# Two row-major projections of a transformer block on one core: the last two chunks by token block

## The reference, cut to what matters

```python
x = x + rms_norm(memory_attention(h, m, w_mq, w_mk, w_mv, w_mo), mem_norm_post)   # ends with "@ w_mo", 1024 x 1024
h = rms_norm(x, ffn_norm_pre)
x = x + rms_norm(conv_ffn(h, w_up, conv_w, conv_b, w_down), ffn_norm_post)        # ends with "@ w_down", 2816 x 1024
...
h = concatenate([meta, x]); u = _rmsnorm(h, norm_w[0]); proj = u @ w_in           # first product of the second model
```

## Time and profile before

| What | Value |
|---|---|
| Median of 3 runs | 923.64 us (923.4 to 923.68) |
| The profiled execution | 922.43 us, of which its span is 920.7 us |
| Granted TensorE clock, mean over the span | 0.999 of full speed |
| PE busy | 908.9 us, 99% of the span |
| DVE, ACT, POOL busy | 655.7, 532.2, 131.6 us |
| Share of PE in the chain of waits that ended last | 93% |

### The profile page before, as it was taken

The page is one execution under the profiler, slowest core; times in us unless marked ns, Lnnn a source line. Parts: engine busy times, 40 slices in busy tenths (PEclk is TensorE's granted clock), DMA queues, the critical chain, the costliest instruction groups (busy, mean ns, idle before and its releaser), DMA issues.

```text
span 920.7 us, 19094 instructions
## 1 busy us (share of the span) xinstructions
PE 908.9 (99%) x6971; PEld 853.1 (93%) x6971; DVE 655.7 (71%) x1115; ACT 532.2 (58%) x904; POOL 131.6 (14%) x131
## 2 busy tenths in 40 slices
PE   8999999999999999999999999999999999999997
PEld 7998899998999998889999999999999998888886
DVE  4898877545899998447877777766578476767743
ACT  6868586545776765546444444444464567666643
POOL 2211010000056566000111111101010000000000
PEclk9999999999999999999999999999999999999999
DMA  8853434435345555652555555555355444455561
GB/s 303 278 169 109 149 109 166 158 117 184 135 161 204 197 193 207 211 203 96 190 174 179 175 174 178 171 196 180 139 184 185 159 159 135 160 166 161 182 196 56
DMA packets 44995, 157.58 MB, mean 171 GB/s; under 512 B 6067, under 2 KB 7219, under 8 KB 44684
## 3 DMA queue, kind: packets, MB, share of 16 engines
q1 hardware_dynamic: 44380, 155.03, 49.4%
q0 software_dynamic: 560, 1.79, 0.7%
HBM read 155.74 MB, written 1.06 MB: 170 GB/s over the span
## 4 chain that ended last, share of the span: by engine, by line
PE 93%; DVE 3%; ACT 2%; issue 1%; DMA 1%; SPq 0%; DVEq 0%; ACTq 0%
PE acc L1311 13%; PE acc L1313 13%; PE acc L1312 13%; PE scores L1311 6%; PE scores L1313 6%; PE scores L1312 6%; PE acc L1264 4%; PE acc L1266 4%; PE acc L1265 4%; PE scores L1265 2%; PE scores L1266 2%; PE scores L1264 2%; PE outs L1266 2%; PE outs L1264 2%; PE outs L1265 2%; PE acc L1395 1%
## 5 line engine op out<-in xcount | busy, mean ns | idle before, releaser
L1884 DVE TENSOR_TENSOR w_lo<-raw,w_hi 128x1024 fp32r<-128x1024 f32 x287 | 353.4, 1238 | 97.0 <-ACT w_hi L665 96.5
L665 ACT ACTIVATE w_hi<-raw 128x1024 fp32r<-128x1024 f32 x287 | 301.3, 1056 | 150.4 <-PE acc L1313 62.7
L1311 PE MATMUL acc<-XH,w_hi 128*128 128x256 f32 (+1 forms) x616 | 176.2, 286 | 0.5 <-DVE Y L2431 0.3
L1312 PE MATMUL acc<-XL,w_hi 128*128 128x256 f32 (+1 forms) x616 | 173.5, 282 | 0.0
L1313 PE MATMUL acc<-XH,w_lo 128*128 128x256 f32 (+1 forms) x616 | 173.5, 282 | 0.0
L1311 PE MATMUL scores<-XH,w_hi 128*128 128x272 f32 (+1 forms) x424 | 120.1, 283 | 0.0
L1313 PE MATMUL scores<-XH,w_lo 128*128 128x272 f32 (+1 forms) x424 | 119.7, 282 | 0.0
L1312 PE MATMUL scores<-XL,w_hi 128*128 128x272 f32 (+1 forms) x424 | 119.7, 282 | 0.0
L1311 PEld LDWEIGHTS acc<-XH,w_hi 128*128 128x128 f32 x616 | 115.9, 188 | 3.0 <-issue 2.4
L1312 PEld LDWEIGHTS acc<-XL,w_hi 128*128 128x128 f32 x616 | 116.0, 188 | 0.1
L1313 PEld LDWEIGHTS acc<-XH,w_lo 128*128 128x128 f32 x616 | 115.9, 188 | 0.0
(11 more groups left out here) (539 smaller groups left out, 1801.7 us busy)
## 6 DMA issues: line engine op xcount, KB each, us to landing
raw<-weights SPq DMA_DIRECT2D x287, 512.0 KB, 3.4
cst<-params SPq DMA_DIRECT2D x1, 1080.5 KB, 10.7
XR<-x_t SPq DMA_DIRECT2D x2, 512.0 KB, 6.1
Y<-mem_t SPq DMA_DIRECT2D x1, 1024.0 KB, 9.6
AR<-bias_rows POOLq DMA_DIRECT2D x4, 256.0 KB, 5.4
out<-AR SPq DMA_DIRECT2D x2, 512.0 KB, 2.6
AR<-final_gain POOLq DMA_DIRECT2D x1, 512.0 KB, 6.1
AR<-lgate_w POOLq DMA_DIRECT2D x1, 192.0 KB, 2.6
```

Source lines behind the costliest of these rows:

```text
L665: nc.scalar.activation(w_hi[:, n % SLOTS, :], raw[:, n % SLOTS, :], ACT.Copy).then_inc(hi_ready, 1)
L1311: nc.tensor.matmul(o, wh, h, start=start, stop=False)
L1312: nc.tensor.matmul(o, wh, l, start=False, stop=False)
L1884: V.tensor_tensor(w_lo[:, s, :], raw[:, s, :], w_hi[:, s, :].bitcast(F32), ALU.subtract).then_inc(lo_ready, 1)
```

## The change

It has five parts, in the memory output and in the down projection alike.

1. **PE, last two chunks by block.** Of the second half's last two chunks, block 0's twelve products are made first, then block 1's twelve. `rows_half` rises behind block 0's. `chunk_done` of both chunks is raised in block 1's part.
2. **PE, the two matmuls of `keep_warm(WARM, PTB)` between the products and the transposes are gone** (4 records of the profile for each stage). The two behind the transposes stay.
3. **ACT, `hi` of the chunk three behind the stage's last** (the next stage's third chunk) stands behind block 0's root instead of ahead of block 0's squares.
4. **POOL makes the low part of that chunk** (`lo_behind`) in place of DVE; DVE hands it on with a one-column memset that raises `lo_ready`. In the down projection it stands ahead of the gate weights' loading on POOL's queue.
5. **DVE adds tiles 0 and 1 of the residual by block**: block 0's 128 columns as soon as they are turned (`first_turned`), ahead of block 1's reciprocal, and block 1's 128 columns behind it. Two semaphores are merged with others.

```diff
--- before.py
+++ after.py
@@ -341,8 +341,9 @@
         rf_zero, sum_ready, cmp_hidden, cmp_copied, rest_pool = (
             sem("rf_zero"), sem("sum_ready"), sem("cmp_hidden"), sem("cmp_copied"), sem("rest_pool"))
         rel_loaded = sem("rel_loaded")
-        gate_loaded, gate_scaled, gate_summed, l_gate_summed, gate_parted = (
-            sem("gate_loaded"), sem("gate_scaled"), sem("gate_summed"), sem("l_gate_summed"), sem("gate_parted"))
+        first_turned, behind_lo = sem("first_turned"), sem("behind_lo")
+        gate_scaled, gate_summed, gate_parted = (
+            sem("gate_scaled"), sem("gate_summed"), sem("gate_parted"))
         token_rstd, shifted, rf_ready, rf_hi, gate_exp, swapped = (
             sem("token_rstd"), sem("shifted"), sem("rf_ready"), sem("rf_hi"), sem("gate_exp"),
             sem("swapped"))
@@ -609,6 +610,15 @@
 
             sum_squares(lambda m: wait_evacuated(pool, TILE["w_out"] + m), META)
 
+            def lo_behind(name, per):
+
+                n = CHUNK[name] + 2 * per - 1 + AHEAD
+                w = n % SLOTS
+                pool.wait_ge(hi_ready, n + 1)
+                nc.gpsimd.tensor_tensor(w_lo[:, w, :], raw[:, w, :], w_hi[:, w, :].bitcast(F32), ALU.subtract).then_inc(behind_lo, 1)
+
+            lo_behind("mo", 4)
+
             def ffn_pool(p, i, hidden, rest):
                 pool.wait_ge(f_gelu, p + 1 + 2 * i)
                 pool.wait_ge(u_tapped, 2 * p + 2 + 4 * i)
@@ -622,8 +632,9 @@
             for p in range(16, FFN_TILES):
                 ffn_pool(p, 0, ffn_hi(p), ffn_lo(p))
 
-            pool.dma_start(lgate_raw, lgate_w).then_inc(gate_loaded, 16)
-            pool.wait_ge(gate_loaded, 16)
+            lo_behind("down", FFN_TILES // 2)
+            pool.dma_start(lgate_raw, lgate_w).then_inc(row_loaded, 16)
+            pool.wait_ge(row_loaded, 16)
             w = grouped(lgate_raw)
             nc.gpsimd.tensor_tensor(w, w, col("g_mlstm", 0, KT).unsqueeze(2).to_broadcast([P, KT, STRIP]), ALU.mult).then_inc(gate_scaled, 1)
             for v in (gA, gA_tail, rstd_m[:, S:T]):
@@ -720,7 +731,7 @@
             def rows_norm(name, u, per):
 
                 n, t = CHUNK[name], TILE[name]
-                for c in range(2 * per):
+                for c in range(2 * per - 1):
                     ahead(n + c)
                     if c == per:
                         wait_chunk(act, n + per - 1)
@@ -732,6 +743,7 @@
                     if b == 0:
                         act.wait_ge(rows_half, u + 1)
                     else:
+                        ahead(n + 2 * per - 1)
                         wait_chunk(act, n + 2 * per - 1)
                     chain.link(nc.scalar.activation(sqv[:, span(2 + b, 512)], SC[:, span(b, 512)], ACT.Square,
                                                     accum_out=row_sq2[:, b:b + 1]))
@@ -1061,7 +1073,7 @@
             for m in range(KT):
                 ahead(CHUNK["lq"] + m)
                 if m == 0:
-                    act.wait_ge(l_gate_summed, 1)
+                    act.wait_ge(gate_summed, 2)
                     nc.scalar.activation(gx[0:36, :], OB[1][0:36, 0:T], ACT.Identity, bias=col("gate_b")[0:36]).then_inc(g_raw, 1)
                     act.wait_ge(g_raw, 1)
                     chain.link(nc.scalar.activation(ge[32:36, :], gx[32:36, :], ACT.Abs))
@@ -1270,7 +1282,7 @@
                 t = TILE[name]
                 for half in range(2):
                     o = [acc(t + b)[:, :] if half == 0 else SC[:, span(b, 512)] for b in range(2)]
-                    for c in range(per):
+                    for c in range(per if half == 0 else per - 2):
                         n = CHUNK[name] + per * half + c
                         pe.wait_ge(lo_ready, n + 1)
                         if half == 0:
@@ -1280,10 +1292,18 @@
                                 pe.wait_ge(evacuated[(t + b) % 2], (t + b) // 2)
                             for j in (2 * c, 2 * c + 1):
                                 last = rows_product(n, o[b], x, j, b, j == 2 * per - 1, j == 0)
-                            if half and b == 0 and c == per - 1:
-                                last.then_inc(rows_half, 1)
                         last.then_inc(chunk_done, 1)
-                keep_warm(WARM, PTB)
+                for b in range(2):
+                    for c in (per - 2, per - 1):
+                        n = CHUNK[name] + per + c
+                        if b == 0:
+                            pe.wait_ge(lo_ready, n + 1)
+                        for j in (2 * c, 2 * c + 1):
+                            last = rows_product(n, o[b], x, j, b, j == 2 * per - 1)
+                        if b:
+                            last.then_inc(chunk_done, 1)
+                    if b == 0:
+                        last.then_inc(rows_half, 1)
                 for b in range(2):
                     for k in range(KT):
                         if b == 0 and k == 0:
@@ -1297,6 +1317,8 @@
                         last = nc.tensor.transpose(turned_rows(k)[:, b * P:(b + 1) * P], y_rows[:, b, k * P:(k + 1) * P], ident[:, :])
                         if b and k % 2:
                             last.then_inc(rows_turned, 1)
+                        elif k == 1:
+                            last.then_inc(first_turned, 1)
                 keep_warm(WARM_SPREAD)
 
             def begin(n, t, first, i=0, depth=2):
@@ -1732,7 +1754,7 @@
                     stat_sum(NORM_H1, 2, lambda: pe.wait_ge(sq_ready, SQ_H1 + KT), T)
                 if m == 3:
                     pe.wait_ge(gate_parted, 1)
-                    nc.tensor.matmul(OB[1][:, 0:T], lgate_raw[:, KT * STRIP:KT * STRIP + P], lgate_parts, start=True, stop=True).then_inc(l_gate_summed, 1)
+                    nc.tensor.matmul(OB[1][:, 0:T], lgate_raw[:, KT * STRIP:KT * STRIP + P], lgate_parts, start=True, stop=True).then_inc(gate_summed, 1)
             for m in range(KT):
                 chunk(CHUNK["lq"] + m, TILE["lq"] + m, l_in(AH, META), l_in(AL, META), S, ready=h1_ready if m == 0 else None)
                 if m == 6:
@@ -1959,8 +1981,18 @@
             def rows_update(name, u, update, post, pre, a):
 
                 t = TILE[name]
+
+                def add_block(k, b):
+                    cols = slice(META + b * P, META + (b + 1) * P)
+                    return V.scalar_tensor_tensor(out=XR[:, k, cols], in0=turned_rows(k)[:, span(b, P)], scalar=col(post, k),
+                                                  in1=XR[:, k, cols], op0=ALU.mult, op1=ALU.add)
+
                 for b in range(2):
                     rstd_b = row_rstd[:, b:b + 1]
+                    if b:
+                        dve.wait_ge(first_turned, u + 1)
+                        for k in (0, 1):
+                            add_block(k, 0)
                     dve.wait_ge(rows_root, 2 * u + b + 1)
                     V.reciprocal(rstd_b, row_root[:, b:b + 1]).then_inc(rows_rstd, 1)
                     dve.wait_ge(rows_rstd, 2 * u + b + 1)
@@ -1974,8 +2006,11 @@
                     V.scalar_tensor_tensor(out=XR[:, k, META:T], in0=turned_rows(k), scalar=col(post, k), in1=XR[:, k, META:T],
                                            op0=ALU.mult, op1=ALU.add).then_inc(x_updated, 1)
 
-                add(0)
-                add(1)
+                dve.wait_ge(rows_turned, 4 * u + 1)
+                for k in (0, 1):
+                    add_block(k, 1).then_inc(x_updated, 1)
+                dve.wait_ge(behind_lo, u + 1)
+                V.memset(small[:, 159:160], 0.0).then_inc(lo_ready, 1)
                 for k in range(KT):
                     if k + 2 < KT:
                         add(k + 2)
@@ -2599,7 +2634,7 @@
                 if c == 1:
                     l_lo(LHEADS - 1)
                 if c == 10:
-                    dve.wait_ge(row_loaded, 16)
+                    dve.wait_ge(row_loaded, 32)
                     dve.wait_ge(half_squared, 2)
                     chain.note(V.tensor_scalar(small[:, 44:46], small[:, 40:42], 1.0 / D, EPS, ALU.mult, ALU.add))
                     for b in range(2):
```

## The result

| | median of the runs | ratio to the kernel before, interval |
|---|---|---|
| before | 923.5 us (22 runs, mostly 922.85 to 924.18) | |
| changed | 927.57 us (22 runs, 923.07 to 929.85) | 1.0025, 1.0013 to 1.0037 |

The kernel became slower by 0.25%, where 0.06% faster was forecast, and 927.57 us lies outside the range. (The ratio weighs all runs; that of the two medians alone would be 1.0044.) Both numbers hide something: the changed kernel's 22 times stand in two groups with nothing in between, nine from 923.07 to 923.74 (median 923.33) and thirteen from 927.46 to 929.85 (median 927.81). The profiled execution, 927.71 us with a span of 926.0, is of the upper group.

A forecast was written before the change was run, and what follows sets the result against it. The prediction took PE, busy 99% of the span, as the bound. Gains of 0.15 and 0.13 us made 0.27 us per seam, 0.54 us for two, taking 923.64 to 923.1 us; range 922.2 to 924.4.

The forecast's parts named there:

- signs of being right: Both seams about 3.5 us, hole 0.7 to 1.0, reciprocal 0.04 behind root, POOL's low part 2.3 to 3.0 us.
- signs of being wrong: PE's first product released by DVE's memset or POOL, clock below 1.00 at either seam, or a seam under 3 us.
- What bounds the kernel: Whole kernel: PE is busy 99% of the span, so gains must come from PE's own instructions or idle time.
- Order of the products, keep_warm, hole: Seam: block 0's transposes begin 0.88 us earlier, leaving a hole before block 1's; by themselves these 0.88 us give nothing.
- Reciprocal 0.15 us earlier: Seam, block 1: DVE is free sooner, so its reciprocal and PE's transposes come 0.15 us earlier.
- Additions by block 0.13 us: Seam's end: half-tile additions bring ACT's high part forward, meeting the second keep_warm's end; first product another 0.13 us earlier.
- The sum 0.27 for each seam: Memory output and down projection: next stage's first product on PE comes 0.27 us earlier in each.
- POOL's low part, 2.7 us: Seam: POOL's 1024-column subtraction takes 2.7 us, free of DVE contention, over before DVE needs it.
- Rival A: Seams: POOL's subtraction late at 6.6 us, PE starts 3.0 us later in each, 929.6 us; chance 6%.
- Gate weights behind it: Down projection: POOL's gate-weight work may delay DVE by up to 0.74 us, covered by 1.3 us, nothing on the path.
- Rival B: Seams: clock falls to half in the new hole, 1.9 us lost in each, 926.9 us; chance 3%.
- are all that the change can move: Memory output and down projection: only the stretches from PE's last product to next stage's first, 3.78 us, can change.

The follow-up runs named there:

- experiment 8: Changed kernel with the two short keep_warm matmuls between products and transposes put back; 927.74 us, ratio 1.0033.
- 11: Changed kernel plus a one-column POOL memset behind the memory output's low part, minus the two keep_warm matmuls behind the transposes; 922.7 us, ratio 0.9993.
- 1: Kernel before plus one idle one-column POOL memset ahead of the feed-forward loop; 924.38 us, ratio 1.0021.
- 3: Changed kernel with the memory output's low part back on DVE and its residual additions by whole tile; 922.84 us, ratio 0.9995.
- 5: Changed kernel plus one idle one-column POOL memset behind the memory output's low part; 923.0 us, ratio 0.9996.
- 9: Kernel before plus two idle one-column POOL memsets ahead of the feed-forward loop; 923.41 us, ratio 0.9998.
- 2: Kernel before without the one short keep_warm matmul pair ahead of the feed-forward loop; 927.21 us, ratio 1.0037.
- 6: Changed kernel plus three idle one-column POOL memsets behind the memory output's low part; 927.26 us, ratio 1.0038.
- 7: Changed kernel with both moved low parts on DVE and residual tiles added whole; 923.34 us, ratio 1.0001.
- 10: Repeat of the changed kernel plus one idle one-column POOL memset behind the memory output's low part; 922.64 us, ratio 0.9992.
- 4: Changed kernel plus one short keep_warm matmul pair in the feed-forward's third round, two rounds written out; 927.09 us, ratio 1.0048.

## Why the prediction was wrong

None of the prediction's signs of being right failed, and none of its signs of being wrong appeared: they all lie in the seams, and the seams did what they were to do. The time was lost elsewhere.

*What bounds the kernel.* Right, and not followed to its end: at 99% on PE's line, whatever makes a thousand matmuls 4% longer outweighs a seam. I read idle time and clock, and took a matmul's duration as fixed by its form.

*Order of the products, keep_warm, hole.* Right: block 0's transposes follow directly, hole 0.93 us (0.7 to 1.0 forecast). "By themselves they give nothing" was wrong: experiment 8 shows 0.13 us in each seam. The working of the 0.15 us used additions at 229.22, which the seam only has without keep_warm, so the sum held and the share was booked to the wrong part.

*Reciprocal 0.15 us earlier.* Measured 0.15 at the transposes (1.98 against 2.13 us behind the last product), reciprocal 0.04 us behind the root. *Additions by block 0.13 us.* Measured 0.13 to 0.14 (3.63 against 3.50). *The sum 0.27 for each seam*: measured 0.28 and 0.27. The argument that the second keep_warm's end meets the high part made no difference: without it the seam is the same (11).

*POOL's low part, 2.7 us.* Measured 2.36 and 2.35, so the 2.7 was 0.34 us too long, and the four pieces of 256 columns behind it (2.95) 0.59. The estimate from the Trainium skill's "GPSIMD Engine Reference", section "3.1 Elementwise — side-by-side cycle accounting", 2.25 us, was 0.11 too short and so nearer. Nobody waits for it. Rival A did not occur.

*Gate weights behind it.* Right: PE's three chunks behind the down seam last 9.05 us before and after, and DVE's first low part keeps its distance from the seam (429.58 - 423.78 = 424.30 - 418.50 = 5.80).

*Rival B.* The clock is 1.00 in the seam. It did not occur either, though its price of some 4 us came, by another way and at another place.

**The failed step** is the sentence that the seam and its twin "are all that the change can move", and with it the part "The low part on POOL": the instruction was costed by its duration and its neighbours in the seam, and then taken as free. That instruction also shifts the loop behind it in POOL's stream. POOL's second multiplication of the loop comes 0.33 us late, the order at the shared port turns, DVE's low part takes 1.77 us instead of 1.22, and PE waits 0.6 us (shown by experiments 1, 3, 5 and 9). Behind the wait 13 of 22 executions, by their times, ran on in the 117.8 ns rhythm and lost about 4 us more (2 and 6 show that price without the 0.6 us wait). No rival had this chain. The other nine, median 923.33 us, lie near the 923.1 forecast by luck: the seams' 0.55 us and a wait of 0.6 would cancel (no profile shows one of the nine). Where the wait is avoided, the rest of the prediction stands: 923.0 and 922.64 us against the 923.1 forecast.

Not settled: what POOL does in the 0.33 us. Fetching of instructions would be a guess, and the one thing the traces hold on it does not decide: each has a single 8 KB load on the instruction queue q14 in these rounds (for which engine, it does not say), and it starts 4.2 us behind POOL's first multiplication in the kernel before and in the changed one alike, 2.7 us behind it in experiments 5 and 9.

Not settled either: what decides the rhythm behind an interruption. After the wait of 0.6 us 13 of 22, 4 of 12 and 4 of 7 runs were in the upper group (changed kernel, 1, 8), after 0.1 us 5 of 5 (6); without a wait 1 of 66 (3, 5, 7, 9, 10, 11) and 3 of 96 of the kernel before. Experiments 2 and 4 were there in all 5 runs each, 2 without a wait and 4, in its profile, behind the added pair.

## What to carry to other kernels

Where one engine's line is the whole time, count what it does per microsecond in a long stretch before and after (matmuls in a window), not only its gaps: a matmul's pace is not fixed by its shape, and a short interruption can cost far more than its length. An instruction that is put ahead of a loop on a side engine is not free because it is hidden where it stands; look at the first rounds of the next loop for who gets the shared port. Signs of being right or wrong that all lie where the edit is cannot catch such a loss: name one for the stretches in between. And where a time falls into two groups, try the kernel with one idle instruction more before judging the idea.

## What the hardware showed that I had not expected

- Back-to-back 256-column matmuls, each with its weight load, have two rhythms at a granted clock of 1.00: 113.3 and 117.8 ns. Either can last over 100 us (444 against 427 matmuls in 50 us), and in the profiles it changes at an interruption: a wait of 0.1 or 0.6 us, or a short pair, which left the shorter rhythm at one place and the longer one at another.
- One more instruction on POOL, even a one-column memset some 20 us ahead of a loop, makes one step of the loop's first rounds 0.33 us late; two do not; four (the low part and three memsets) make another step 0.38 us late.
- A 128 x 1024 subtraction takes POOL 2.36 us, undisturbed by DVE work that reads PSUM, 1.9 times DVE's 1.23.
